# A hybrid decoder step on one core: the first 50 microseconds written anew

## The reference, cut to what matters

```
h = rmsnorm(x, norm1_g)                     # 264 x 2048
p = h @ w_in                                # 2048 x 18448, split into q, k, v, r, alr (16 columns), cb, cc, cx, ga, gb
loga = log_sigmoid(alr @ w_alpha_up + b_alpha) / 16
... gated linear attention, a short convolution, gates, x = x + m @ w_out
x = x + peer(rmsnorm(x, norm2_g), ...)      # 8 heads x 16 experts per token, gathered from 16384 rows of 8 KB
```

## Time and profile before

| what | value |
|---|---|
| median of 3 runs | 2395.32 us |
| profiled execution, its own time | 2394.96 us |
| its span, first to last instruction | 2392.9 us |
| TensorE busy / weight loads | 1798.2 us / 1275.9 us |
| VectorE, ScalarE, POOL busy | 1601.2, 598.1, 930.4 us |
| mean DMA rate | 325 GB/s |

### The profile page before, as it was taken

One profiled execution on the slowest core, in us unless ns is written; L12 is line 12 of the kernel. 1 busy time (PEld: TensorE's weight loads), 2 busy tenths in 40 slices (PEclk: granted clock), 3 DMA queues, 4 the chain that ended last, 5 costly groups with the idle time before them and its releaser, 6 DMA issues.

```text
span 2392.9 us, 23881 instructions
## 1 busy us (share of the span) xinstructions
PE 1798.2 (75%) x9151; PEld 1275.9 (53%) x9151; DVE 1601.2 (67%) x2021; ACT 598.1 (25%) x869; POOL 930.4 (39%) x729
## 2 busy tenths in 40 slices
PE   7999999999999999986756565655564455755654
PEld 5999889899899899874422222222221121112221
DVE  4544455646555554386778887879887787687765
ACT  4433554645545543301100000100010010010000
POOL 0000111110111100062655666657656666567662
PEclk9999999999999999998887768778767678887677
DMA  6665787878877767599999999999999999999997
GB/s 185 172 173 165 217 245 234 238 221 232 238 229 218 231 197 188 157 394 378 420 421 422 422 422 421 422 422 395 422 422 422 422 421 422 422 406 413 422 422 301
DMA packets 424341, 777.24 MB, mean 325 GB/s; under 512 B 14024, under 2 KB 344288, under 8 KB 355568
## 3 DMA queue, kind: packets, MB, share of 16 engines
q0 software_dynamic: 89168, 597.86, 60.9%
q1 hardware_dynamic: 333792, 175.71, 27.2%
q10 hardware_dynamic: 1272, 2.18, 0.2%
HBM read 754.51 MB, written 21.25 MB: 324 GB/s over the span
## 4 chain that ended last, share of the span: by engine, by line
PE 46%; DMA 30%; DVE 8%; POOL 8%; issue 5%; ACT 3%; another core or an unknown queue 1%; ACTq 0%; DVEq 0%; POOLq 0%; SPq 0%
DMA ring<-in_expert_v,idx_all 29%; PE bank L1476 11%; PE bank L1477 10%; PE bank L1478 10%; PE bank L1656 8%; POOL ring L640 8%; PE bank L1633 2%; DVE x_tok L1310 2%; DVE ring L1292 2%; ACT w_hi L671 1%; DMA ring<-in_expert_v,idx_s 1%; PE bank L1576 1%; PE bank L1557 1%; PE bank L1462 1%
## 5 line engine op out<-in xcount | busy, mean ns | idle before, releaser
L1656 PE MATMUL bank<-ring,diag 128*128 128x512 f32 x1000 | 670.8, 833 | 489.9 <-DMA ring<-in_expert_v,idx_all 427.0
L1292 DVE CUSTOM_DVE_ANT_0 ring<-ring,xn_tok 128x2048 f32<-128x2048 f32 x256 | 583.6, 2290 | 239.7 <-DMA ring<-in_expert_u,idx_all 232.2
L1656 PEld LDWEIGHTS bank<-ring,diag 128*128 128x128 f32 x1000 | 259.2, 272 | 893.9 <-issue 824.3
L1476 PE MATMUL bank<-act_hi,w_hi 128*128 128x264 f32 x2304 | 663.7, 288 | 1.5 <-DVE w_lo L984 1.5
L1477 PE MATMUL bank<-act_lo,w_hi 128*128 128x264 f32 x2304 | 654.3, 284 | 0.0
L1478 PE MATMUL bank<-act_hi,w_lo 128*128 128x264 f32 x2304 | 653.6, 284 | 0.0
L984 DVE TENSOR_TENSOR w_lo<-raw,w_hi 128x2048 fp32r<-128x2048 f32 x144 | 330.2, 2293 | 347.1 <-ACT w_hi L671 346.7
L640 POOL DMA_INDIRECT ring<-in_expert_u,idx_all x256 | 429.7, 1679 | 287.2 <-DVE g_all L1286 106.5
L640 POOL DMA_INDIRECT ring<-in_expert_v,idx_all x256 | 376.4, 1470 | 299.5 <-PE bank L1656 227.8
L1476 PEld LDWEIGHTS bank<-act_hi,w_hi 128*128 128x128 f32 x2304 | 435.1, 189 | 20.7 <-issue 18.3
L1477 PEld LDWEIGHTS bank<-act_lo,w_hi 128*128 128x128 f32 x2304 | 435.7, 189 | 1.0 <-issue 1.0
(11 more groups left out here) (230 smaller groups left out, 1161.8 us busy)
## 6 DMA issues: line engine op xcount, KB each, us to landing
raw<-in_w_in SPq DMA_DIRECT2D x129, 1024.0 KB, 6.6
s_ring<-in_state_gla POOLq DMA_DIRECT2D x64, 256.0 KB, 6.1
out<-s_ring POOLq DMA_DIRECT2D x64, 256.0 KB, 5.9
raw<-in_w_out SPq DMA_DIRECT2D x16, 1024.0 KB, 6.2
raw<-in_w_query SPq DMA_DIRECT2D x9, 1024.0 KB, 28.2
v_row<-v_samples POOLq DMA_DIRECT2D x32, 256.0 KB, 6.2
xslot<-in_w_query SPq DMA_DIRECT2D x7, 1024.0 KB, 10.5
ring<-in_expert_u,idx_all POOLq DMA_INDIRECT x256, 13.9
```

Source lines behind the costliest of these rows:

```text
L1292: v.tensor_tensor_reduce(ring[k][:], ring[k][:], xn_tok[:, b // PH, :], 1.0, 0.0, ALU.mult, ALU.add, w_all[:, b * TOPK + s:b * TOPK + s + ...
L1476: mm(out, hi_, act_hi[:, k, :], start=(k == 0), stop=False)
L1656: ins = mm(bank[sum_bank(t) + j][:], diag[nth % N_DIAG][:], ring[k][:, j * 512:(j + 1) * 512], start=first, stop=final)
```

## The change

All of it lies in the opening, apart from a new order of the parameter columns in `pcol` and a wait.

- **Loads.** SyncE issues the first prompt tile, the second in two halves, then `raw0` and `raw1` at once; the 16 semaphore increments that stood first come after `raw0`. `wau` is loaded four times, at rows 0, 32, 64 and 96. `krow`, `crow` and the copy of the convolution state come after `raw3`. ScalarE's own queue issues the samples and 6 loads of parameter rows in place of 23.
- **Samples.** They are loaded as 128 rows of 128 channels (`xs_flat`). ScalarE squares them in one small operation, a product with a block matrix `same_s` sums 16 rows per sample, and one transpose turns them all.
- **Norm.** ScalarE squares the first prompt tile, VectorE the second, half by half. One activation table serves squares and roots. The scaling is split: VectorE scales channels 0 to 1023 in pieces of 512, POOL channels 1024 to 2047.
- **Clock.** TensorE makes 16, 16 and 4 matmuls of the identity with itself (`warm`) while it waits.
- **Block 0** becomes `rank_rows`: raw fp32 weights of 32 columns, four strips of the array for four k at once, 4 groups of 8 matmuls; the strips' sums are added by the product with the fourfold `wau`, whose contraction now is over 128 rows. ScalarE and VectorE no longer round this block.
- **Block 1** is rounded and multiplied in two halves (`first_queries`).
- The four transposes for `convT` and `keysT` now stand behind the 8 products with `wau`, with a wait for VectorE's last reading of these.

```diff
+            act.dma_start(xs_flat[:], x_sample.rearrange("b s (c p) -> (b s c) p", p=P)).then_inc(xs_in, 16)
+            for r, rows in ((80, norm1_g), (80 + KT, norm2_g), (80 + 2 * KT, b_alpha), (0, gla_norm_g),
+                            (KT, conv_w.rearrange("o j c -> (o j) c")), (4 * KT, conv_b)):
...
+            act.wait_ge(chain, 3)
+            a.activation(root[:], mean_sq[:], ACT.Sqrt).then_inc(rt_done, 1)
+            act.wait_ge(xs_in, 16)
+            a.activation(xs_junk[:], xs_flat[:], ACT.Square, accum_out=xs_part[:, 0:1]).then_inc(xs_ss, 1)
+            act.wait_ge(x_in[0], 16)
+            a.activation(sq_junk[0][:], x_tok[:, 0, :], ACT.Square, accum_out=ssq[:, 0:1]).then_inc(ss_done, 1)
...
+            act.sem_inc(hi_done, 1)
+            act.wait_ge(raw_in[1], 16)
+            a.activation(w_hi[1][:, 0:KT // 2, :], raw[1][:, 0:KT // 2, :], ACT.Copy).then_inc(hi_half, 1)
+            a.activation(w_hi[1][:, KT // 2:KT, :], raw[1][:, KT // 2:KT, :], ACT.Copy).then_inc(hi_done, 1)
...
+                dve.wait_ge(x_in[1], 16)
+                v.tensor_tensor_reduce(sq_junk[1][:, 0:half], x_tok[:, 1, 0:half], x_tok[:, 1, 0:half], 1.0, 0.0, ALU.mult,
+                                       ALU.add, ssq[:, 1:2]).then_inc(x1_ss, 1)
...
+                for part in range(2):
+                    cols_ = slice(part * 512, (part + 1) * 512)
+                    for t in range(2):
+                        v.tensor_scalar(x_tok[:, t, cols_], x_tok[:, t, cols_], rstd[:, t:t + 1], None,
+                                        ALU.mult).then_inc(xn_done, 1)
...
+            pool.wait_ge(rs_done, 1)
+            for part in (2, 3):
+                cols_ = slice(part * 512, (part + 1) * 512)
+                for t in range(2):
+                    g.tensor_scalar(x_tok[:, t, cols_], x_tok[:, t, cols_], rstd[:, t:t + 1], None,
+                                    ALU.mult).then_inc(xp_done, 1)
...
+                dve.wait_ge(mm_done, 1)
+                dve.sem_inc(lo_done, 1)
+                dve.wait_ge(hi_half, 1)
+                v.tensor_tensor(w_lo[1][:, 0:KT // 2, :], raw[1][:, 0:KT // 2, :], w_hi[1][:, 0:KT // 2, :].bitcast(F32),
+                                ALU.subtract).then_inc(lo_half, 1)
...
+            def rank_rows(g):
+                pe.wait_ge(al_done, 4 * g + 4)
...
+                for part, act_ in enumerate((act_hi, act_lo)):
+                    for x in range(4):
+                        k = 4 * g + x
+                        ins = mm(bank[ACC][STRIP * x:STRIP * x + STRIP, 0:T], raw[0][:, k, 0:STRIP], act_[:, k, :].bitcast(F32),
+                                 start=(g == 0 and part == 0), stop=(g == KT // 4 - 1 and part == 1))
...
+            def warm(n):
+                for _ in range(n):
+                    mm(bank[7][:, 0:P], ident[:], ident[:], start=True, stop=True)
...
+            for k in range(KT):
+                turn(k)
...
+                if k == 11:
+                    rank_rows(0)
+                if k == 14:
+                    rank_rows(1)
+            rank_rows(2)
+            rank_rows(3)
+            pe.wait_ge(par_ready, 1)
+            first_queries()
-            turn(0, [x_tok] * 3)
-            project(0, parts_from=0)
-            project(B_Q)
...
+            pe.wait_ge(la_ev, H * KD)
+            pe.wait_ge(conv_in, 16)
+            pe.wait_ge(keys_in, 16)
+            for h in range(2):
+                tr(bank[4][:, h * P:(h + 1) * P], crow[:, h, :], ident[:])
```

More of the change, by code:

```diff
@@ L161, in hybrid_step @@
         convT = sb("convT", [P, KT, 2 * TS])
+        at_flat = where[0]
         oT = sb("oT", [P, HV, T])
@@ L171, in hybrid_step @@
         kv_even = sb("kv_even", [P, DV])
+        at_tA = where[0]
         tA = [sb(f"tA{s}", [P, T]) for s in range(2)]
@@ L447, in _ @@
         def _(sp):
[L448 to L474, removed]
+            sp.dma_start(x_tok[:, 0, :], x_p[:, 0, :]).then_inc(x_in[0], 16)
+            for half in range(2):
+                part = slice(half * (D // 2), (half + 1) * (D // 2))
+                sp.dma_start(x_tok[:, 1, part], x_p[:, 1, part]).then_inc(x_in[1 + half], 16)
             def load(n0, src, i=0, L=0):
@@ L539, in _ @@
             ones_where(ident[:], [[-1, P]], 0, 1)
+            same = same_s[:].rearrange("p (s c) -> p s c", s=TS)
+            made(g.memset(same_s[:], 1.0))
+            for sign, base in ((-1, 0), (1, KT - 1)):
+                pool.wait_ge(consts, n)
+                made(g.affine_select(out=same, in_=same, compare_op=ALU.is_ge, fill=0.0, base=base,
+                                     pattern=[[sign * KT, TS], [0, KT]], channel_multiplier=-sign))
             ones_where(eye8[:], [[1, TS], [-1, TS]], 0, 0)
@@ L1000, in act_parts @@
+            def act_parts():
+                xs = xs_g[:].rearrange("p (c s) -> p c s", s=TS)
+                dve.wait_ge(par_ready, 1)
                 for k in range(KT):
[L1001 to L1004, removed]
+                    dve.wait_ge(ah_done, k + 1)
+                    v.scalar_tensor_tensor(out=act_lo[:, k, 0:TP], in0=bank[2 + k % 6][:, 0:TP],
+                                           scalar=pcol[:, 80 + k:81 + k],
+                                           in1=act_hi[:, k, 0:TP].bitcast(F32),
@@ L1011, in _ @@
             v.memset(q_sel[:], 0.0).then_inc(chain, 1)
[L1012 to L1015, removed]
-            lo(1)
+            N0 = 7
+            dve.wait_ge(chain, N0)
+            norm()
+            act_parts()
             lo(2)
@@ L1070, in head_step @@
                 q = cg * 2 + half
-                par = lambda z: pcol[:, 20 * i + z:20 * i + z + 1]
+                par = lambda z: pcol[:, z + 4 * i:z + 4 * i + 1]
                 lo(n0 + 2)
@@ new lines, in first_queries @@
+            def first_queries():
+                for half in range(2):
+                    if half == 0:
+                        pe.wait_ge(lo_half, 1)
+                    else:
+                        pe.wait_ge(lo_done, 2)
+                    for k in range(half * KT // 2, (half + 1) * KT // 2):
+                        out = bank[ACC + 1][:, 0:T]
+                        mm(out, w_hi[1][:, k, :], act_hi[:, k, :], start=(k == 0), stop=False)
+                        mm(out, w_hi[1][:, k, :], act_lo[:, k, :], start=False, stop=False)
+                        ins = mm(out, w_lo[1][:, k, :], act_hi[:, k, :], start=False, stop=(k == KT - 1))
+                ins.then_inc(mm_done, 1)
```

201 lines of the change are left out of this document (128 added, 73 removed).

## The result

The changed kernel takes 2358.09 us (2357.01 to 2369.67, 4 runs) against 2395.22 us; the ratio is 0.9853, with a 95% interval of 0.9825 to 0.988. That is 37 us less, where 10.9 were forecast. The forecast of 2384.4 us and its range, 2379 to 2391, both missed.

What follows compares the result with a forecast made beforehand. The prediction took TensorE to bound the kernel before 1021 us and DMA from 1200 us, with only the opening ahead changed: 11.9 - 1.5 + 0.5 = 10.9 us less, giving 2384.4 us, range 2379 to 2391.

Steps and rivals of the forecast that it cites:

- the last sentence of its first paragraph: Gathers' stage: begins when the TensorE-bound stage ends, its bytes stay the same, so an earlier first dense block moves all behind.
- The sum: Opening's terms: 11.9 us gained by block 1's end, minus 1.5, plus 0.5 for the clock, 10.9 us in all.
- The first turn: First transpose of tokens in the opening: starts at 12.0 us, 7.6 us earlier, bounds 11.5 and 19.6 us.
- a first turn that waits for VectorE beyond 13 us: Opening: a sign that would show the prediction wrong; the first turn was forecast at 12.0 us.
- Turns and strips: Token transposes and block 0's strip matmuls: 14.1 us, 6.0 of it strips; strips end at 26.1 us, 13.9 earlier.
- Block 1: Second block: 1.35 us idle, 48 matmuls in 5.8 us, 0.8 for a low clock; ends at 34.0 us, 11.9 earlier.
- Behind the products: After the 8 decay products: 0.5 us wait and 1.0 us transposes delay block 2 by 1.5; clock regains 0.5.
- the likeliest case's own range: Whole kernel: the forecast case, chance 0.78, from 2380 us (clock high throughout) to 2388 us (strips 8.0, clock low at block 1).
- A shift that shrinks behind 100 us: After the opening: a sign of being wrong; each event from block 2 to the end should come 11 us earlier.
- The identity matmuls don't raise the clock: Rival for the opening: clock stays low, turns start at 19.6 us, kernel takes 2395.1 us; chance 0.08.
- Strips in series: Rival for block 0: strips run one behind the other at the low clock, 30.6 us, kernel 2410 us; chance 0.05.
- Half of it goes elsewhere: Rival: late second tile, slow POOL pieces over 2.5 us or the gathers leave 5 us of gain, 2390 us; chance 0.09.

## Why the prediction was wrong

**The step that failed** is the last sentence of its first paragraph: that all behind the first dense block only moves, because the gathers' "bytes stay the same". They did, but their rate did not: it rose from 422 to 427 GB/s. The gathers' 597.9 MB differ by 16.6 us between these two rates, and the stage took 21.5 us less in the profiled execution of the kernel with 96 bytes more, which is 18.6 us less in the median. Part of the rest lies before 1200 us, where the query weights are loaded beside the gathers: from 1020 to 1200 us the windows add up to 74.1 MB in place of 71.9. The prediction had read that the DMA engines were busy all the time at 413 GB/s, and so that the rate sets the length of this stage; what it missed is three lines of the change, the new tiles ahead of `act_hi`. The sum prices the instructions of the change and no address, so the term for the gathers stood at nothing, with the bytes as its only reason. This one omission is worth 18.6 of the 37 us, and with it the sum would have been 10.9 + 18.6 = 29.5. No row that the prediction uses gives its size.

The sum starts from 2394.96 us, a time that no run listed here has; those of the kernel before lie within 0.5 us of it.

**The first turn**, 12.0 us forecast, came at 13.14. The identity matmuls ended at 12.35, as reckoned (12.4); VectorE was late:

```profile
8.44 1.23 DVE L1013 CUSTOM_DVE_ANT_0 sq_junk<-x_tok 128x1024 f32<-128x1024 f32 x1 [5.21 <-DMA x_tok<-in_x_prompt]
...
9.86 1.23 DVE L1021 CUSTOM_DVE_ANT_0 sq_junk<-x_tok 128x1024 f32<-128x1024 f32 x1
...
11.77 1.32 DVE L1035 TENSOR_SCALAR x_tok<-x_tok,rstd 128x512 f32<-128x512 f32 x2
```

Each half square took 1.23 us (1.15 priced), but the first half had landed only by 8.4 us, so both stood in series behind it and were done at 11.1, where 9.9 was reckoned; and the pieces took 0.66 us beside POOL, not 0.35. The prediction had named a first turn that waits for VectorE beyond 13 us as a sign of being wrong, and it came.

**Turns and strips**, 14.1 us forecast, took 11.1. Strips side by side was right: 1.1 us a group, the lower bound. The middle of 6.0 us between the two clocks was too careful by 1.6, as the clock did not fall in this stretch; the other 1.4 us are turns that went quicker than the 8.1 us reckoned.

**Block 1**: 1.55 us of idle TensorE (1.35 forecast), then 48 matmuls at 0.12 us throughout. The 0.8 us for a low clock was not needed.

**Behind the products**: forecast 1.5 us of waits and transposes. From the first product to block 2 the changed kernel takes 4.7 us (31.61 to 36.33), the one with the transposes moved 3.4 (31.77 to 35.13): 1.4 us for the term, of which 1.1 are left at block 6 and at the gathers. The clock's 1.5 us came in full at block 6, where 0.5 was counted, and was lost again by 235 us.

Together the opening gave 13.4 us at block 2, 14.9 at block 6 and 13.35 at the first gather, against 10.9: right in kind and 2.5 us low, at the edge of the likeliest case's own range, which the kernel with the old addresses (2381) confirms. A shift that shrinks behind 100 us was the other sign of being wrong, and it came too: 14.8 us at the first `stage` transpose (136.8 us for 151.6), 13.3 from the heads on (257.4 for 270.7), because of the clock's fall at 231 us.

**The rivals.** "The identity matmuls don't raise the clock" was wrong as put, and so was the use that the forecast made of them: they do raise it (the first 16 take 5.96 us, the next 16 take 3.82), and it is of no use, as block 2 comes no later without them. Strips in series fell by their first row. "Half of it goes elsewhere" named late landings and POOL's pieces; POOL took 1.7 us a piece, within the 2.5 us that were allowed.

## What to carry to other kernels

A change of a kernel is also a change of its addresses. Where a stage is bound by DMA into SBUF, look at the start of its tiles before pricing anything else, and try them on multiples of 256 bytes: here that was 0.8% for 96 unused bytes. Price a stage that you take to be merely moved by its rate as well. For TensorE's clock, look for instructions of few rows before you fill a wait with matmuls of no use: here transposes and products over 128 rows brought the clock up or kept it up where those over 8 and 16 did not. And follow a gain to the end of the trace: the 1.5 us won from the clock behind block 1 were lost to the clock at 231 us.

## What the runs showed of the hardware

- Rows of 512 bytes into SBUF: 291 GB/s with starts 160, 192 or 128 bytes past a multiple of 256 (291, 291 and 293), 347 on one. Rows of 8 KB: 421 to 422 against 427.
- Transposes of 128 rows raised TensorE's clock; with every third of 8 rows, and 0.33 us ahead of each, it stayed low for 13 us, and the first block began at 0.22 us a matmul. At the end of 3.8 us of products over 16 rows it fell, at the end of the same over 128 rows, the added weights zero, it did not.
- Behind a pause of 1.75 us of TensorE at the same place of the program the clock fell to 0.50 for some 3 us in the changed kernel, and stayed up in the kernel before.
- Four strips of 32 columns side by side: eight fp32 instructions with 264 columns of data in 0.45 us from start to start (18.68 to 19.13), and 0.58 us from the last strips to the start of the transposes behind them (19.13 to 19.71).
- VectorE's scaling of 512 columns takes 0.48 us alone and 0.78 beside POOL's, and POOL's 1.69 beside VectorE's.
